# Taking the squares of x behind the rounding of all eight tiles in block 2

## The reference

```
u = rms_norm(h, mix_pre_g[i]);  y = mixer(u)              # dilated (layer 0), differential attention (layer 1)
h = h + rms_norm(y, mix_post_g[i])
u = rms_norm(h, mem_pre_g[i])
y = memory_cross_attention(u, rms_norm(mem, mem_kv_g[i]), x_wq[i], x_wkv[i], x_wo[i])
h = h + rms_norm(y, mem_post_g[i])
u = rms_norm(h, ffn_pre_g[i])
y = swiglu_ffn(u, w_gate_up[i], w_down[i])
h = h + rms_norm(y, ffn_post_g[i])
```

## Time and profile before

| what | us |
|---|---|
| median of 3 runs | 3390.35 (3390.07 to 3393.16) |
| the profiled execution, its own time | 3389.65 |
| its span | 3387.8 |
| PE busy | 3124.5 (92%) |
| DVE busy | 1877.8 (55%) |
| ACT busy | 1265.9 (37%) |
| POOL busy | 348.1 (10%) |

### The profile page before, as it was taken

How to read it: one execution, slowest core, us unless ns; L and a number is a source line. 1 busy time by engine, 2 the same in 40 slices (tenths; PEclk the granted TensorE clock), 3 DMA queues, 4 the chain that set the end, 5 groups by cost and what they waited for, 6 DMA issues and landing times.

```text
span 3387.8 us, 37313 instructions
## 1 busy us (share of the span) xinstructions
PE 3124.5 (92%) x14560; PEld 2427.2 (72%) x14560; DVE 1877.8 (55%) x2604; ACT 1265.9 (37%) x2009; POOL 348.1 (10%) x260
## 2 busy tenths in 40 slices
PE   7898899998998899998998997999799889979997
PEld 5677788886677788885666866888656458668886
DVE  6755543467755544466665646444667647464445
ACT  6634322245634322344444333222333423332222
POOL 2000100022000100022001202000210013020001
PEclk9998999999988999999999999999999989989998
DMA  3110233222111222321112312232211113122332
GB/s 133 44 44 32 82 99 97 96 96 72 50 38 41 81 100 94 99 94 61 50 50 82 123 45 69 99 97 96 69 56 56 38 62 131 44 69 95 98 99 76
DMA packets 73723, 259.08 MB, mean 76 GB/s; under 512 B 8020, under 2 KB 10200, under 8 KB 73176
## 3 DMA queue, kind: packets, MB, share of 16 engines
q1 hardware_dynamic: 72824, 252.99, 22.8%
q0 software_dynamic: 736, 3.87, 0.3%
HBM read 254.73 MB, written 2.10 MB: 76 GB/s over the span
## 4 chain that ended last, share of the span: by engine, by line
PE 57%; issue 25%; DVE 10%; ACT 3%; POOLq 2%; DVEq 1%; DMA 0%; ACTq 0%; POOL 0%
PE bank L496 42%; DVE w_lo L1759 3%; POOLq L2531 2%; PE bank L987 2%; PE bank L998 1%; ACT w_hi L1154 1%; PE bank L704 1%; PE bank L557 1%; PE bank L1008 1%; PE bank L545 1%; PE bank L1012 1%; PE bank L1024 1%; PE bank L743 1%; PE bank L766 1%; PE bank L731 1%
## 5 line engine op out<-in xcount | busy, mean ns | idle before, releaser
L496 PE MATMUL bank<-a_hi,w_hi 128*128 128x512 f32 x2040 | 829.7, 407 | 96.0 <-DVE a_lo L1789 46.3
L496 PE MATMUL bank<-a_hi,w_lo 128*128 128x512 f32 x2040 | 803.6, 394 | 0.0
L496 PE MATMUL bank<-a_lo,w_hi 128*128 128x512 f32 x2040 | 803.1, 394 | 0.0
L1759 DVE TENSOR_TENSOR w_lo<-w_raw,w_hi 128x1024 fp32r<-128x1024 f32 (+1 forms) x474 | 632.3, 1335 | 280.9 <-ACT w_hi L1154 279.7
L496 PE MATMUL bank<-b_hi,w_hi 128*128 128x512 f32 (+1 forms) x1688 | 646.5, 383 | 49.0 <-DVE w_lo L1759 21.0
L1154 ACT ACTIVATE w_hi<-w_raw 128x1024 fp32r<-128x1024 f32 (+1 forms) x474 | 494.3, 1044 | 419.0 <-DMA w_raw<-weights 418.8
L496 PE MATMUL bank<-b_lo,w_hi 128*128 128x512 f32 (+1 forms) x1688 | 636.9, 377 | 0.0
L496 PE MATMUL bank<-b_hi,w_lo 128*128 128x512 f32 (+1 forms) x1688 | 636.2, 377 | 0.0
L496 PEld LDWEIGHTS bank<-a_hi,w_hi 128*128 128x128 f32 x2040 | 388.8, 191 | 209.8 <-issue 67.1
L496 PEld LDWEIGHTS bank<-a_lo,w_hi 128*128 128x128 f32 x2040 | 389.5, 191 | 85.9 <-issue 7.9
L496 PEld LDWEIGHTS bank<-a_hi,w_lo 128*128 128x128 f32 x2040 | 388.4, 190 | 83.8
(11 more groups left out here) (280 smaller groups left out, 3040.7 us busy)
## 6 DMA issues: line engine op xcount, KB each, us to landing
w_raw<-weights SPq DMA_DIRECT2D x458, 512.0 KB, 3.4
w_raw<-weights SPq DMA_DIRECT2D x16, 384.0 KB, 2.9
x<-x SPq DMA_DIRECT2D x8, 256.0 KB, 7.2
mem<-mem POOLq DMA_DIRECT2D x2, 1024.0 KB, 5.0
out<-x SPq DMA_DIRECT2D x8, 256.0 KB, 2.0
mem<-mem SPq DMA_DIRECT2D x1, 1024.0 KB, 12.0
ple<-ple POOLq DMA_DIRECT2D x2, 512.0 KB, 3.8
o<-c_level SPq DMA_DIRECT2D x1, 512.0 KB
```

The source lines that it names most:

```text
L496: last = mm(bank[G_BANK[u % 4] if at is None else at][:, 0:cols], w[:, u % SLOTS, ks], t[:, k, 0:cols], start=(k == 0 and n == 0), stop=(k ...
L1759: tt(w_lo[:, u % SLOTS, w], w_raw[:, u % SLOTS, w], f32(w_hi[:, u % SLOTS, w]), ALU.subtract).then_inc(w_lo_ready, 1)
```

## The change

In `kv`, ACT now rounds the eight tiles during the first eight units without squaring, and squares them during the second eight, one behind each step; that loop is written out. POOL makes the eight additions to x first (`add_scaled`) and the eight square additions after them. In `post`, ACT rounds all eight tiles and then squares all eight; POOL and DVE keep their order there. In block 1's gate stage POOL's loop is written in another way with the same instructions in the same order. PE's and DVE's programs are untouched.

```diff
@@ -1194,12 +1194,12 @@
                 c.groups += 1
                 f(root[:, 0:cols], bank[SUM_BANK][:, 0:cols], ACT.Sqrt, bias=eps, scale=1.0 / D).then_inc(root_ready, 1)
 
-            def round_x(dst, k, gain, wait=True):
-
-                if wait:
-                    act.wait_ge(x_ready, c.count(x_ready))
+            def round_x(dst, k, gain, squared=True):
+
+                act.wait_ge(x_ready, c.count(x_ready))
                 f(dst[0][:, k, :], x[:, k, :], ACT.Copy, scale=gain).then_inc(a_hi_ready, 1)
-                square(x[:, k, :])
+                if squared:
+                    square(x[:, k, :])
 
             def values(n, tok=ST):
                 for i in range(n):
@@ -1606,7 +1606,9 @@
                 root_of_mean()
                 for k in range(8):
                     if name is not None:
-                        round_x(a_op, k, col(name[0], name[1], k))
+                        round_x(a_op, k, col(name[0], name[1], k), squared=False)
+                for k in range(8 if name is not None else 0):
+                    square(x[:, k, :])
 
             def ahead(limit):
 
@@ -1671,10 +1673,10 @@
                 root_of_mean()
                 for k in range(8):
                     step()
-                    round_x(a_op, k, col("mem_pre", l, k))
-                with c.loop(2, {}, 4):
-                    for _ in range(4):
-                        step()
+                    round_x(a_op, k, col("mem_pre", l, k), squared=False)
+                for k in range(8):
+                    step()
+                    square(x[:, k, :])
 
             def xq(l):
                 split_and_root()
@@ -2515,29 +2517,29 @@
                 pool.wait_ge(met["act"], c.count(met["act"]))
                 pool.wait_ge(met["dve"], c.count(met["dve"]))
 
-            def add_squares(cols=S, before=None):
+            def add_squares(cols=S):
                 for k in range(8):
-                    if before is not None:
-                        before(k)
-                    n = c.squares
-                    pool.wait_ge(sq_ready, c.count(sq_ready))
-                    s = sq[:, n % 2, 0:cols]
-                    if k == 0:
-                        if c.groups > 0:
-                            pool.wait_ge(sum_ready, c.groups)
-                        pool.tensor_copy(sq_sum[:, 0:cols], s).then_inc(sq_added, 1)
-                    else:
-                        pool.tensor_tensor(sq_sum[:, 0:cols], sq_sum[:, 0:cols], s, ALU.add).then_inc(sq_added, 1)
-                    pool.drain()
-                    c.squares += 1
+                    add_square(k, cols)
                 c.groups += 1
 
-            def ahead(k, made, tile):
-
-                for j in ([0, 1] if k == 0 else [k + 1]):
-                    if j < 8:
-                        pool.wait_ge(made, c.count(made))
-                        pool.tensor_tensor(x[:, j, :], x[:, j, :], y[:, tile + j, :], ALU.add).then_inc(x_ready, 1)
+            def add_square(k, cols=S):
+                n = c.squares
+                pool.wait_ge(sq_ready, c.count(sq_ready))
+                s = sq[:, n % 2, 0:cols]
+                if k == 0:
+                    if c.groups > 0:
+                        pool.wait_ge(sum_ready, c.groups)
+                    pool.tensor_copy(sq_sum[:, 0:cols], s).then_inc(sq_added, 1)
+                else:
+                    pool.tensor_tensor(sq_sum[:, 0:cols], sq_sum[:, 0:cols], s, ALU.add).then_inc(sq_added, 1)
+                pool.drain()
+                c.squares += 1
+
+            def add_scaled(made, tile):
+
+                for j in range(DT):
+                    pool.wait_ge(made, c.count(made))
+                    pool.tensor_tensor(x[:, j, :], x[:, j, :], y[:, tile + j, :], ALU.add).then_inc(x_ready, 1)
 
             def load(l):
                 add_squares()
@@ -2574,7 +2576,8 @@
                 pool.dma_start(mem[:, :, :], dram["mem"].rearrange("p (a b) -> p a b", a=DT)).then_inc(mem_landed, 16)
                 add_squares()
 
-                add_squares(before=lambda k: ahead(k, y_scaled, 0))
+                add_scaled(y_scaled, 0)
+                add_squares()
 
             def cross(l):
                 meet()
@@ -2601,7 +2604,14 @@
                 out1(l)
                 add_squares()
                 add_squares()
-                add_squares(before=lambda k: ahead(k, e_gated, 8))
+                pool.wait_ge(e_gated, c.count(e_gated))
+                pool.tensor_tensor(x[:, 0, :], x[:, 0, :], y[:, 8, :], ALU.add).then_inc(x_ready, 1)
+                for k in range(DT):
+                    if k + 1 < DT:
+                        pool.wait_ge(e_gated, c.count(e_gated))
+                        pool.tensor_tensor(x[:, k + 1, :], x[:, k + 1, :], y[:, 9 + k, :], ALU.add).then_inc(x_ready, 1)
+                    add_square(k)
+                c.groups += 1
 
             pool.wait_ge(x_ready, DT * 3 * LAYERS)
             pool.dma_start(dil[:, :], dram["c_dilated"]).then_inc(dil_landed, 16)
```

## The result

The changed kernel takes 3395.05 us (median of 20 runs, 3389.64 to 3402.73) against 3390.29 us for the one before (20 runs): ratio 1.0015, 95% interval [1.0008, 1.0022]. It is 0.15% slower, 5 us. That is less than the 0.2% that the prediction calls no change, but the interval lies above 1, so these runs tell it from none: the change costs 2.7 to 7.5 us. The forecast was 3391.6, with 3382 to 3401 around it.

What follows compares the result with a forecast made beforehand. Most of the span was put on PE's own instructions, so the change counts only where PE waits: -9.4 us in the stages and +10.6 in the passes give +1.2, so 3391.6 us, with 3382 to 3401 as the whole range.

Steps and rivals of the forecast that it cites:

- The mechanism of the stage: Key and value stage, first eight units: without POOL's square additions, DVE's y scaling falls from 1.45 to 0.74 us.
- Its size: Key and value stage: steps fall from 4.53 to 3.9 us, unit 9 starts 4.7 us sooner, 9.4 us over both layers.
- The tail of the stage: Key and value stage from unit 9: PE is the bound, so everything behind moves along and the 4.7 us stay.
- The passes: Three post passes: DVE freed sooner, but sum later and PE's clock lowered; together 10.6 us lost.
- the relief: Post passes: DVE's add of x falls from 1.78 to 0.69 us, so the last rounding ends 6.8 us sooner.
- the later sum: Post passes: eight squares in a row take 11.5 us, so PE's sum starts 1.8 us later.
- The clock penalty: Two ffn_pre passes: after standing still 9 us PE runs at half clock, losing 2.2 us a pass.
- The rule of the lock: End of ffn_pre passes: DVE's weight split and POOL's last square addition exclude each other; if DVE won, sum 1.2 us later.
- Full gain of PE's waits: Rival, key and value stage: all of PE's waits for w_lo go, -17.7 us, total 3383.2; chance 0.13.
- The load's pace: Rival, post passes: POOL's additions in a row take 1.54 us or more, 3.0 us more a pass, 3400.5; chance 0.12.
- A pass that isn't freed: Rival, post passes: x's slow add isn't due to POOL, squares start no sooner, 20.4 us more, 3412; chance 0.09.
- Weights as the bound: Rival, key and value stage: DMA of weights limits the first eight units, no gain there, 3401; chance 0.05.

Runs made afterwards that it cites:

- short additions in the old order: The kernel before, but in the key and value stage POOL adds only the first 8 columns of each square; 3384.20 us, ratio 0.9981.
- Short additions: The kernel before, but in the three post passes POOL adds only the first 8 of 512 columns of each square; 3371.89 us, ratio 0.9947.
- one unit ahead of the sum: Changed kernel, but mix_pre pass as before and PE doing one more unit before the sum in the ffn_pre passes; 3382.12 us, ratio 0.9975.

## Why the prediction came out as it did

The total was right within its range, and the case named likeliest, a change within 0.2%, is the one that came. There is luck in that: against a sum of +1.2 us the traces have +3.4, made of stages 1.6 us better than put, a loss of 4.4 us behind them that no term had, -0.2 us in the passes and -0.4 us in layer 1's mixer. By its steps:

*The mechanism of the stage* (a collision with POOL's square additions in each of DVE's steps) was right: short additions in the old order win 5.1 and 5.0 us of the 5.6 and 5.4. *Its size* was low. The step is 3.83 us where 3.9 was put, and unit 9 starts 5.4 us sooner instead of 4.7; together -11.0 us instead of -9.4. The part that was mis-sized is the last: up to the fourth step DVE is ahead by 2.2 us (2.0 put), the three ordinary steps give the 2.1 us put, and the step without additions gives 1.1 instead of 0.6 us.

*The tail of the stage* was taken to move as a whole, and it does to the next root. That the gain is kept behind it was never asked, and this is the step that failed: +4.4 us over two layers, in the cross attention, where PE's clock fell in layer 0 and fell for longer in layer 1. The prediction priced the clock where it added a standstill, and not where it only moved one. The trace of before holds one layer with the clock up through the attention and one with it down, and the same work takes 124.2 us (root at 1922.47 to root at 2046.67) in the one and 127.8 us (2858.73 to 2986.49) in the other: a warning of 3.6 us that stood there to be read.

*The passes*: 10.6 us put, 10.4 us measured (2.72 + 0.50, 2.76, 3.89 + 0.49). Of the two terms the relief was right, and the later sum in layer 0. Short additions show the relief of DVE to be 6.7 us (6.8 put), and the sum comes 27.56 - 25.90 = 1.66 us later in layer 0 (1.8 put). The clock penalty of 2.2 us a pass was high: 10 matmuls in 4.40 us were put at half clock, but in layer 0 the window behind the sum has a mean of 0.66, since part of it was granted in full: the slower sum (1.05 us) and the ffn behind it (0.50) come to 1.6 us. That is some 1.3 us less over two passes, and what made it up to 10.4 is the next point, so the good fit of this sum is luck in part.

*The rule of the lock* decided one pass of two. In layer 0 POOL's last addition began first (2079.29) and DVE's split at 2079.34 took 2.29 us. In layer 1 the split came first, and the addition ran on to 3022.60:

```profile
3020.25 1.23 DVE L1761 TENSOR_TENSOR w_lo<-w_raw,w_hi 128x1024 fp32r<-128x1024 f32 x1 [9.28 <-ACT w_hi L1154]
```

```profile
3020.49 2.11 POOL L2534 TENSOR_TENSOR sq_sum<-sq_sum,sq 128x512 f32<-128x512 f32 x1 [0.45 <-issue]
```

```profile
3022.64 2.08 PE L523 MATMUL bank<-sq_sum,der 128*128 128x512 f32 x2 [9.47 <-POOL sq_sum L2534]
```

That is the 1.1 us between the passes' 2.7 and 3.9 us. The Trainium skill (SBUF — State Buffer, "Who interferes with whom") has the issue order decide who blocks, and here both outcomes stand in one trace. The prediction gave the price (1.2 us) and left it out of the sum; in one of the two passes it was due.

*The rivals.* Full gain of PE's waits: no, 4.2 and 3.2 us of them are left. The load's pace: no, the additions are 1.43 us apart, first to last 2079.29 - 2069.88 = 9.41 us. A pass that isn't freed: no, x's add is 0.69 us. Weights as the bound: no, the first eight now take 156 GB/s and PE's waits are still for DVE, though ACT waits for transfers for 7.6 us of them, where it was 0.4.

What stays open: why the clock stays up in the attention of layer 0 in all of the traces with the old stage and falls in all with the new one, so long after the stage; what decides on the second fall; and 1.4 us between the traces' +3.4 and the +4.8 of the medians, which is inside the interval.

## What to carry to other kernels

Before work of POOL is put off to free DVE, look for what PE has to do in the meantime: where eight units followed (the key and value stage) the same move won 5.5 us, and where the sum was asked for next (the post passes) the 6.7 us saved were paid back with 9 to 12 us, so a change with two such places should be timed at each alone. The part that wins is worth some 7 us (0.2%) by itself, and with needless products before the attention or one unit ahead of the sum 3380 to 3382 us were measured, the fastest of the kernels here that leave nothing out. Count the gain to the end of the next stretch with a half-idle PE, not to the end of its own.

## What the runs showed of the hardware

In layer 0 PE's clock fell to 0.50 behind a standstill of 2.4 us in the seven traces whose stage before was some 5.5 us shorter, and stayed at 1.00 behind the same 2.4 us in the three without that. Ten needless matmuls in the standstill kept it at 1.00 there in both layers of all three kernels that had them, and cost 0.8 us where it would have stayed up anyway. A stretch of identical instructions (layer 0's mixer of block 1) varied over 7.8 us between traces, from -1.42 to +6.39 us against before, while the stages and passes repeat to 0.1 us between two traces of one kernel. An addition of 512 columns on DVE takes 0.69 us alone and 1.78 us beside one of POOL.
